# Two-block transformer on one core: positions loaded as columns, the compressing network's gelu written out with tanh, banded turns three steps later

## The chip, the cores and the metric

The kernel runs on one core of a Trainium2 chip, as five hand-written engine programs: TensorE (PE), VectorE (DVE), ScalarE (ACT), GpSimd (POOL) and SyncE (SP), which issues most of the DMAs. The metric is the device time of one execution in microseconds; lower is better.

## The reference

512 tokens of width 1024 in fp32 pass through two two-layer blocks. A layer of the first block mixes banded attention, a pooling mixer and MLA attention (which turns queries and keys by the positions), then a gated FFN. A layer of the second block has forgetting attention (fox) and sparse attention (NSA), whose compressed keys and values come out of a small network with a gelu.

```python
# first block, per layer; positions are 512 int32
ang = positions.astype(jnp.float32)[..., None] * inv_freq
cos, sin = jnp.cos(ang), jnp.sin(ang)
q_rope = apply_rope(q_rope, cos[:, :, None, :], sin[:, :, None, :])
k_rope = apply_rope(k_rope, cos, sin)
...
# swa_mixer: 6 query heads, 2 key heads, window 128, a bias by distance, sinks
q = rms_norm(q.reshape(B, S, SWA_HEADS, HEAD_DIM), q_gain)
k = rms_norm(k.reshape(B, S, SWA_KV_HEADS, HEAD_DIM), k_gain)
...
# second block, per layer, for keys (0) and values (1)
def compress_blocks(t, pos_emb, w1, b1, w2, b2):
    ...
    flat = blocks.reshape(B, G, nc, CMP_BLOCK * dh)
    return jax.nn.gelu(flat @ w1 + b1) @ w2 + b2
```

## The kernel before, in words

**Main parts and sides.** TensorE does every large product in fp32 as three matmuls of split parts (lines 667 to 669: high by high, low by high, high by low). A weight unit is loaded by SP into RAW, ScalarE makes the high part Wh (line 1520), VectorE the low part Wl (line 2283), both ahead of their use. Beside these main parts run "sides": generators for the small work (turns, i.e. transposes on TensorE, norms, attention items, the compressing network). At each step of the main part `tick` advances every open side to its next `yield`; `idle(n)` lets n steps go by. So the numbers in `idle` decide where in each engine's queue a small operation stands, and each engine works through its queue strictly in order. PSUM's eight banks go round: `fresh` waits until the bank's last reader is done (`bankN_drained`), a reader waits for `bankN_full`.

**Positions and angles.** SP loads the 512 positions as four rows POI[0:4, 128], last of 15 small loads that share the semaphore `gains_in`. VectorE casts them beside the gain rows (L2712), TensorE turns the gain rows (L1048) and the other rows with the positions (L1049), and VectorE copies the result into four columns of SS (L2718). Then VectorE begins the angles (L2743, L2745, L2747 into ANG), POOL carries them on in some 45 dependent operations (L3475 to L3506), with two DMAs of the bias table among them (L3534 waits for VectorE's VB, L2729). ScalarE takes the sine (L1828, L1829), and right behind it in its queue stands the copy of the values, V (L1847), which frees a bank that TensorE's main part waits for.

**POOL's first DMAs** wait for both halves of x (`x_in`), then come the 11 small loads of `small_in`; the last two are `b_forget`. TensorE's bias row (L1058) waits for all 11.

**Banded turns** (`window_side`). In each layer of the first block five 128-wide tiles of doubled keys (KD) and queries (QK) are turned on TensorE (L1032); ScalarE and VectorE take the high and low parts (KH, KL, QP) between MLA's attention items (L888 turns probabilities, L903 multiplies with values).

**The compressing network** (`keys_side(kv)`), in each layer of the second block for keys (kv 0) and values (kv 1): the hidden activations (64 blocks by 256) are turned on TensorE into "ht" (two tiles 128x64), ScalarE applies `Gelu_apprx_tanh` with the bias (L2141) into H1, TensorE multiplies by w2 (L1365). For the keys VectorE copies and rotates the result (KC, L3187 to L3193), TensorE turns it (L1373, "kct"), and KCHL takes its two parts.

Of the kernel before, what the change touches and what calls it, by code (L numbers as in the profile page):

```python
# [12 lines left out]
I32 = mybir.dt.int32  # L13
# [158 lines left out]
class Memory:  # L172

    def __init__(self, nc, ctx):
# [48 lines left out]
        self.POI = area("POI", [P], 9856, I32)  # L224
# [65 lines left out]
        self.H1 = area("H1", [2, 64], 20480)  # L290
        self.W2 = area("W2", [2, 2, 64], 20608)
# [48 lines left out]
class Signals:  # L340

    def __init__(self, nc, ctx):
        def sem(name):
            return ctx.enter_context(nc.semaphore(name))
# [6 lines left out]
        self.small_in = sem("small_in")  # L352
        self.blank = sem("gain_rows_blank")
# [60 lines left out]
        self.rk = sem("nsa_k_turned")  # L414
        self.h1 = sem("cmp_hidden_made")
# [222 lines left out]
N_GAINS, N_SMALL, N_NORMS = 15, 11, 4 * DEPTH  # L638
# [4 lines left out]
def tensor_program(pe, M, G, K, plan):  # L643
# [399 lines left out]
    def gains_side():  # L1043
        yield from idle(9)
        b = fresh("gains")
        pe.wait_ge(G.gains_in, 16 * N_GAINS)
        pe.wait_ge(G.set_up, 4)
        pe.transpose(b[:, 0:G_ROWS], M.GR[0:G_ROWS, :], ident[0:G_ROWS, 0:G_ROWS])  # L1048
        pe.transpose(b[:, 128:128 + 68], M.GR2[0:68, :], ident[0:68, 0:68]).then_inc(*K.fills("gains"))  # L1049
        K.close("gains")  # L1050
        yield from idle(3)
# [48 lines left out]
    def window_side(l):  # L1100
        yield from idle(24)
        while "bias" not in done:
            yield
        for j in (3, 4, 0, 1, 2):
            pe.wait_ge(G.win_k, 4 * l + 4)
            if j < 3:
                pe.wait_ge(G.win_n, NT * l + NT)
                turn_rows(f"win{l} {j}", lambda s: M.QK[:, s, j * P:(j + 1) * P])
            else:
                turn_rows(f"win{l} {j}", lambda s: M.KD[:, s, j - 3, :])  # L1110
            K.close(f"win{l} {j}")
            yield
            yield
# [147 lines left out]
    for l in range(DEPTH):  # L1261
# [89 lines left out]
        def keys_side(kv):  # L1351
            yield from idle(4)
            b = fresh(f"ht{l} {kv}")
            pe.wait_ge(*K.drained(f"hid{l} {kv}"))
            for j in range(2):
                i = pe.transpose(b[:, j * 64:j * 64 + 64], M.HT[0:64, j * P:j * P + P], ident[0:64, 0:64])
            i.then_inc(*K.fills(f"ht{l} {kv}"))
            yield
            K.close(f"ht{l} {kv}")
            yield from idle(3)  # L1360
            b = fresh(f"w2{l} {kv}")
            pe.wait_ge(*K.drained(f"ht{l} {kv}"))
            pe.wait_ge(G.w2_in, 32 * l + 32)
            for j in range(2):
                pe.matmul(b[0:64, 0:64], M.H1[:, j, :], M.W2[:, kv, j, :], start=j == 0, stop=False)  # L1365
            pe.matmul(b[0:64, 0:64], M.ONE[0:1, :], M.B2[0:1, 2 * l + kv, :], start=False, stop=True).then_inc(*K.fills(f"w2{l} {kv}"))
            yield
            if kv == 0:
                K.close(f"w2{l} {kv}")
                yield from idle(4)  # L1370
                b = fresh(f"kct{l}")
                pe.wait_ge(G.kc, l + 1)
                pe.transpose(b[:, 0:64], M.KC[0:64, :, :].rearrange("p a b -> p (a b)"), ident[0:64, 0:64]).then_inc(*K.fills(f"kct{l}"))  # L1373
                yield
# [127 lines left out]
def scalar_program(sc, M, G, K, plan, a):  # L1502
# [314 lines left out]
    def gains_side():  # L1817
        yield from idle(13)
        sc.wait_ge(G.set_up, 7)
# [39 lines left out]
    def window_side(l):  # L1859
        yield from idle(24)  # L1860
# [151 lines left out]
    for l in range(DEPTH):  # L2012
# [120 lines left out]
        def keys_side(kv):  # L2133
# [5 lines left out]
            for j in range(2):  # L2139
                col = G_B1 + 4 * l + 2 * kv + j  # L2140
                i = sc.activation(M.H1[:, j, :], M.bank[K.of(name)][:, j * 64:j * 64 + 64], ACT.Gelu_apprx_tanh, bias=M.GT[:, col:col + 1])  # L2141
            i.then_inc(*K.empties(name))
            yield from idle(4 if kv == 0 else 6)
            if kv == 0:
                yield from idle(5)
                upper(M.KCHL[:, :, 0, :], M.bank[K.of(f"kct{l}")][:, 0:64].rearrange("p (g n) -> p g n", n=32), f"kct{l}")
# [118 lines left out]
def vector_program(ve, M, G, K, plan):  # L2265
# [440 lines left out]
    def gains_side():  # L2706
# [10 lines left out]
        ve.tensor_copy(M.GT[:, G_ROWS:G_ROWS + 64], b[:, 128:192]).then_inc(G.set_up, 1)  # L2717
        ve.tensor_copy(PS4, b[:, 192:196]).then_inc(*K.empties("gains"))  # L2718
# [4 lines left out]
        ve.wait_ge(G.set_up, 7)  # L2723
# [95 lines left out]
    def window_side(l):  # L2819
# [7 lines left out]
        yield from idle(6)  # L2827
# [164 lines left out]
    for l in range(DEPTH):  # L2992
# [188 lines left out]
        def keys_side(kv):  # L3181
            yield from idle(9)
            name = f"w2{l} {kv}"
            b = M.bank[K.of(name)]
            if kv == 0:
# [8 lines left out]
                yield from idle(5)  # L3194
# [183 lines left out]
def sync_program(sp, M, G, K, plan, a, out):  # L3378
# [36 lines left out]
    sp.dma_start(M.POI[0:NT, :], a["positions"].rearrange("a (t p) -> (a t) p", p=P)).then_inc(G.gains_in, 16)  # L3415
# [21 lines left out]
def gpsimd_program(gp, M, G, K, a):  # L3437
# [164 lines left out]
```

## Time and profile before

| | |
|---|---|
| runs, us | 2717.89, 2719.95, 2719.98 (median 2719.95) |
| profiled execution, us | 2718.81 |
| its span, us | 2717.0 |
| PE busy | 2674.8 us, 98% |
| DVE busy | 1521.7 us, 56% |
| ACT busy | 1135.1 us, 42% |
| POOL busy | 210.0 us, 8% |
| TensorE's granted clock | 0.999 of 2.4 GHz |

The span runs from the first to the last instruction of the profiled execution; the time is 1.8 us longer. "Busy" adds up an engine's instructions, without waits. A row of the waits says which instruction waited, for what, how long in total, how many times, and the longest.

### The profile page before, as it was taken

Reading aid. Unit: us, or ns where it says so; the run is one execution under the profiler, and the core shown is the slowest. Engines: PE = TensorE matmul, PEld = TensorE weight load, DVE = VectorE, ACT = ScalarE, POOL = GpSimd, SP = SyncE. Lnnn points to the kernel's source line nnn. Section 1 sums busy time; section 2 is a strip of 40 time slices with the busy share of each in tenths; the row PEclk is TensorE's granted clock in tenths of the full one; section 3 lists DMA queues with packets and bytes.
Section 4 is the critical chain, followed back from the end, with each engine's and each line's share of the span. In section 5 each row is a group of like instructions: output and inputs, shape, how many; then the busy total and the mean of one; then the engine's idle time right before and its main releaser. Section 6 shows DMA issues by size and latency. Waiting matters only on the chain.

```text
span 2717.0 us, 34704 instructions
## 1 busy us (share of the span) xinstructions
PE 2674.8 (98%) x13449; PEld 2217.3 (82%) x13449; DVE 1521.7 (56%) x2678; ACT 1135.1 (42%) x2055; POOL 210.0 (8%) x323
## 2 busy tenths in 40 slices
PE   8999999999999999999999999999999999999999
PEld 7788888887888888878877888888878778888887
DVE  7756444467564444676776653343677776643343
ACT  4644222236542222455655343242465655342232
POOL 5200000002000000021122000000020121000000
PEclk9999999999999999999999999999999999999999
DMA  5113232321132333333311333333333212323332
GB/s 146 36 42 103 93 101 93 101 81 58 34 101 96 98 97 98 93 101 89 114 48 40 98 96 93 101 94 98 109 88 105 79 40 63 104 91 101 93 101 86
DMA packets 192279, 237.70 MB, mean 87 GB/s; under 512 B 12674, under 2 KB 145764, under 8 KB 192116
## 3 DMA queue, kind: packets, MB, share of 16 engines
q1 hardware_dynamic: 188852, 228.04, 27.9%
q0 software_dynamic: 2256, 5.52, 1.0%
q8 instruction: 108, 1.77, 0.3%
q10 hardware_dynamic: 1008, 1.92, 0.2%
q14 instruction: 55, 0.45, 0.0%
HBM read 227.05 MB, written 2.11 MB: 84 GB/s over the span
## 4 chain that ended last, share of the span: by engine, by line
PE 89%; DVE 5%; ACT 2%; POOL 1%; issue 1%; DMA 0%; SPq 0%; ACTq 0%; DVEq 0%; POOLq 0%
PE bank L667 26%; PE bank L669 26%; PE bank L668 26%; PE bank L958 2%; PE bank L903 1%; PE bank L979 1%; PE bank L980 1%; PE bank L1022 1%; PE bank L1021 1%; DVE Wl L2283 1%; PE bank L1223 1%; PE bank L888 1%; PE bank L1032 1%; PE bank L1421 1%; PE bank L1017 0%
## 5 line engine op out<-in xcount | busy, mean ns | idle before, releaser
L2283 DVE TENSOR_TENSOR Wl<-RAW,Wh 128x1024 fp32r<-128x1024 f32 (+4 forms) x434 | 511.5, 1201 | 326.0 <-ACT Wh L1520 325.1
L1520 ACT ACTIVATE Wh<-RAW 128x1024 fp32r<-128x1024 f32 (+4 forms) x434 | 438.1, 1032 | 397.6 <-PE bank L669 392.4
L667 PE MATMUL bank<-Hh,Wh 128*128 128x512 f32 x1104 | 448.3, 406 | 2.2 <-DVE Hl L2353 1.5
L669 PE MATMUL bank<-Hh,Wl 128*128 128x512 f32 x1104 | 431.7, 391 | 0.0
L668 PE MATMUL bank<-Hl,Wh 128*128 128x512 f32 x1104 | 431.0, 390 | 0.0
L667 PE MATMUL bank<-HA,Wh 128*128 128x512 f32 x704 | 274.2, 390 | 0.0
L669 PE MATMUL bank<-HA,Wl 128*128 128x512 f32 x704 | 273.9, 389 | 0.0
L668 PE MATMUL bank<-HA,Wh 128*128 128x512 f32 x704 | 273.9, 389 | 0.0
L669 PEld LDWEIGHTS bank<-Hh,Wl 128*128 128x128 f32 x1104 | 207.2, 188 | 45.0
L667 PEld LDWEIGHTS bank<-Hh,Wh 128*128 128x128 f32 x1104 | 208.3, 189 | 40.6 <-issue 4.8
L668 PE MATMUL bank<-A,Wh 128*128 128x512 f32 x608 | 236.5, 389 | 0.0
L667 PE MATMUL bank<-A,Wh 128*128 128x512 f32 x608 | 236.5, 389 | 0.0
L669 PE MATMUL bank<-A,Wl 128*128 128x512 f32 x608 | 236.5, 389 | 0.0
L668 PEld LDWEIGHTS bank<-Hl,Wh 128*128 128x128 f32 x1104 | 208.1, 188 | 33.6
L669 PEld LDWEIGHTS bank<-HA,Wl 128*128 128x128 f32 x704 | 132.1, 188 | 27.5
L668 PEld LDWEIGHTS bank<-HA,Wh 128*128 128x128 f32 x704 | 132.2, 188 | 27.3
L667 PEld LDWEIGHTS bank<-HA,Wh 128*128 128x128 f32 x704 | 132.1, 188 | 27.3
L2452 DVE TENSOR_TENSOR XT<-bank,XT 128x512 f32<-128x512 f32 x112 | 77.1, 690 | 121.6 <-PE bank L669 121.0
L1738 ACT ACTIVATE P<-bank,STT 128x384 f32<-128x384 f32 (+1 forms) x192 | 101.2, 527 | 96.7 <-DVE STT L2639 95.8
L667 PE MATMUL bank<-Wh,Hh 128*128 128x512 f32 (+3 forms) x384 | 139.4, 363 | 2.2 <-DVE Wl L2283 2.2
L2353 DVE TENSOR_TENSOR A<-TMP,A 128x512 fp32r<-128x512 f32 x108 | 74.8, 693 | 117.9 <-ACT A L1933 87.2
L669 PE MATMUL bank<-Wh,Hl 128*128 128x512 f32 (+3 forms) x384 | 134.6, 350 | 0.0
(408 smaller groups left out, 4711.3 us busy)
## 6 DMA issues: line engine op xcount, KB each, us to landing
RAW<-in_w_up_dram SPq DMA_DIRECT2D x108, 512.0 KB, 3.7
RAW<-in_w_down_dram SPq DMA_DIRECT2D x108, 512.0 KB, 3.7
RAW<-in_w_in_dram SPq DMA_DIRECT2D x86, 512.0 KB, 3.7
RAW<-in_w_gate_dram SPq DMA_DIRECT2D x44, 512.0 KB, 3.7
RAW<-in_w_out_dram SPq DMA_DIRECT2D x28, 512.0 KB, 3.7
RAW<-in_cmp_w_dram SPq DMA_DIRECT2D x16, 512.0 KB, 3.9
RAW<-in_w_o_fox_dram SPq DMA_DIRECT2D x8, 512.0 KB, 4.5
RAW<-in_w_o_nsa_dram SPq DMA_DIRECT2D x8, 512.0 KB, 3.5
```

The source lines that it names most:

```text
L667: pe.matmul(o, sh, mh, start=first, stop=False)
L668: pe.matmul(o, sh, ml, start=False, stop=False)
L669: return pe.matmul(o, sl, mh, start=False, stop=last)
L888: x = pe.transpose(b[:, k * P:(k + 1) * P], M.PB[:, i % 4, k * P:(k + 1) * P], ident)
L903: x = pe.matmul(b[:, h * 64:(h + 1) * 64], M.PT[:, i % 3, k * P:(k + 1) * P], values(g, h, kb[k]), start=k == 0, stop=k == len(kb) - 1)
L958: x = pe.transpose(b[:, k * P:(k + 1) * P], e[:, k * P:(k + 1) * P], ident)
L979: pe.matmul(b[:, c:c + w], v, ph, start=B.opens(n) and k == 0, stop=False, skip_group_check=True)
L1520: sc.activation(M.Wh[:, v % NHL, 0:n], M.RAW[:, v % NRAW, 0:n], ACT.Copy).then_inc(G.w_hi, 1)
L1738: sc.activation(e, M.bank[K.of(name)][:, 0:e.shape[1]], ACT.Exp, bias=M.STT[:, 0, t, h:h + 1], accum_out=M.STT[:, 1, t, h:h + 1]).then_inc ...
L2283: ve.tensor_tensor(M.Wl[:, v % NRAW, 0:n], M.RAW[:, v % NRAW, 0:n], M.Wh[:, v % NHL, 0:n].bitcast(F32), ALU.subtract).then_inc(G.w_lo, 1)
L2353: return ve.tensor_tensor(lo, src, h.bitcast(F32), ALU.subtract)
L2452: ve.tensor_tensor(M.XT[:, k, :], M.bank[K.of(name)][:, :], M.XT[:, k, :], ALU.add).then_inc(*K.empties(name))
```

## The change

It has three parts, which touch different stretches of the program.

1. **Positions.** Four DMAs of POOL load the positions straight into four columns (128 pieces of 4 bytes each), issued between the waits for the first and the second halves of x. The cast now makes the four columns of SS directly, and it and the three first angle operations stand in VectorE's queue ahead of the fourth Wl. The cast L2712, the copy L2718 and one of SP's loads go; the turn of the other rows has 64 rows in place of 68.
2. **Compressing network.** In place of the two gelus ScalarE takes h + b into HX (Identity) and its square into H1 (Square), VectorE makes (0.044715 x² + 1)·x, ScalarE the tanh, VectorE (0.5 t + 0.5)·x. The w2 matmuls and what follows stand later.
3. **Banded turns.** `window_side` begins three steps later on the three engines.

```diff
     def gains_side():          # TensorE
         yield from idle(9)
         pe.wait_ge(G.gains_in, 16 * N_GAINS)          # N_GAINS 15 -> 14
-        pe.wait_ge(G.set_up, 4)
+        pe.wait_ge(G.set_up, 3)
         pe.transpose(b[:, 0:G_ROWS], M.GR[0:G_ROWS, :], ident[0:G_ROWS, 0:G_ROWS])
-        pe.transpose(b[:, 128:128 + 68], M.GR2[0:68, :], ident[0:68, 0:68]).then_inc(*K.fills("gains"))
+        pe.transpose(b[:, 128:128 + 64], M.GR2[0:64, :], ident[0:64, 0:64]).then_inc(*K.fills("gains"))
...
     def window_side(l):        # TensorE, ScalarE; VectorE: idle(6) -> idle(9)
-        yield from idle(24)
+        yield from idle(27)
...
             K.close(f"ht{l} {kv}")   # TensorE, keys_side
-            yield from idle(3)
+            yield from idle(6)
             b = fresh(f"w2{l} {kv}")
-            pe.wait_ge(*K.drained(f"ht{l} {kv}"))
+            pe.wait_ge(G.h1, 2 * l + kv + 1)
...
                 K.close(f"w2{l} {kv}")
-                yield from idle(4)
+                yield from idle(6)
                 b = fresh(f"kct{l}")
...
             for j in range(2):       # ScalarE, keys_side
                 col = G_B1 + 4 * l + 2 * kv + j
-                i = sc.activation(M.H1[:, j, :], M.bank[K.of(name)][:, j * 64:j * 64 + 64], ACT.Gelu_apprx_tanh, bias=M.GT[:, col:col + 1])
+                h = M.bank[K.of(name)][:, j * 64:j * 64 + 64]
+                sc.activation(M.HX[:, j, :], h, ACT.Identity, bias=M.GT[:, col:col + 1])
+                i = sc.activation(M.H1[:, j, :], h, ACT.Square, bias=M.GT[:, col:col + 1])
             i.then_inc(*K.empties(name))
-            yield from idle(4 if kv == 0 else 6)
+            yield from idle(2)
+            sc.wait_ge(G.h_in, 2 * l + kv + 1)
+            sc.activation(M.H1[:, :, :], M.H1[:, :, :], ACT.Tanh, scale=float((2.0 / np.pi) ** 0.5)).then_inc(G.h_tanh, 1)
+            yield from idle(5 if kv == 0 else 7)
             if kv == 0:
-                yield from idle(5)
+                yield from idle(7)
...
     def gains_side():          # VectorE
-        yield from idle(7)
-        ve.wait_ge(G.gains_in, 16 * N_GAINS)
-        ve.tensor_copy(M.GR2[64:64 + NT, :], M.POI[0:NT, :]).then_inc(G.set_up, 1)
-        yield from idle(3)
+        yield from idle(10)
...
-        ve.tensor_copy(PS4, b[:, 192:196]).then_inc(*K.empties("gains"))
...
     def angle_side():          # VectorE
-        yield from idle(10)
+        yield from idle(3)
-        ve.wait_ge(*K.drained("gains"))
+        ve.wait_ge(G.pos_in, 16 * NT)
+        ve.tensor_copy(PS4, M.POI[:, :]).then_inc(*own.up())
+        ve.wait_ge(*own.now())
...
         def keys_side(kv):     # VectorE
-            yield from idle(9)
+            yield from idle(6)
+            ve.wait_ge(*K.drained(f"ht{l} {kv}"))
+            ve.tensor_scalar(M.H1[:, :, :], M.H1[:, :, :], 0.044715, 1.0, ALU.mult, ALU.add).then_inc(*own.up())
+            ve.wait_ge(*own.now())
+            ve.tensor_tensor(M.H1[:, :, :], M.H1[:, :, :], M.HX[:, :, :], ALU.mult).then_inc(G.h_in, 1)
+            yield from idle(2)
+            ve.wait_ge(G.h_tanh, 2 * l + kv + 1)
+            ve.tensor_scalar(M.H1[:, :, :], M.H1[:, :, :], 0.5, 0.5, ALU.mult, ALU.add).then_inc(*own.up())
+            ve.wait_ge(*own.now())
+            ve.tensor_tensor(M.H1[:, :, :], M.H1[:, :, :], M.HX[:, :, :], ALU.mult).then_inc(G.h1, 1)
+            yield from idle(4)
...
     for s in range(NT):        # POOL
-        for half in range(2):
-            gp.wait_ge(G.x_in[s][half], 16)
+        gp.wait_ge(G.x_in[s][0], 16)
+    for t in range(NT):
+        gp.dma_start(M.POI[:, t:t + 1], a["positions"][0, t * P:(t + 1) * P].rearrange("(p o) -> p o", o=1)).then_inc(G.pos_in, 16)
+    for s in range(NT):
+        gp.wait_ge(G.x_in[s][1], 16)
```

**Order, place 1.** VectorE's queue near the start, of before, from its copy of the diagonal masks (CMB) on; the first piece left out holds the low parts of x (Hl) and copies of its turned tiles (XT), the second also 13 small operations of the first norm.

```order
L2709 CAST CMB_65<-CST_61 128x128
L2283 TENSOR_TENSOR Wl_53<-RAW_52,Wh_54 128x832 [waits weights_hi_made]
...
L2712 CAST GR_31_79<-POI_80 4x128 [waits gains_in]
L2283 TENSOR_TENSOR Wl_53<-RAW_52,Wh_54 128x1024 [waits weights_hi_made]
...
L2718 COPY SS_71<-bank 128x4
L2720 TENSOR_SCALAR GT_62<-GT_62 128x2 [waits vector_own]
L2721 TENSOR_SCALAR GT_62<-GT_62 128x2
L2743 TENSOR_TENSOR ANG_81<-SS_71,CST_61 128x64 [waits bank1_drained]
L2745 TENSOR_SCALAR ANG_81<-ANG_81 128x64 [waits vector_own]
L2747 TENSOR_TENSOR ANG_81<-ANG_81 128x64 [waits vector_own]
L2729 TENSOR_TENSOR VB_76<-bank,INI_77 6x384 [waits bank2_full]
```

The same place of the change:

```order
L2718 CAST CMB_65<-CST_61 128x128
L2749 CAST SS_71<-POI_80 128x4 [waits positions_in]
L2751 TENSOR_TENSOR ANG_81<-SS_71,CST_61 128x64 [waits vector_own]
L2753 TENSOR_SCALAR ANG_81<-ANG_81 128x64 [waits vector_own]
L2755 TENSOR_TENSOR ANG_81<-ANG_81 128x64 [waits vector_own]
L2292 TENSOR_TENSOR Wl_53<-RAW_52,Wh_54 128x832 [waits weights_hi_made]
...
L2726 TENSOR_SCALAR GT_62<-GT_62 128x2 [waits vector_own,bank1_drained]
L2727 TENSOR_SCALAR GT_62<-GT_62 128x2
L2735 TENSOR_TENSOR VB_76<-bank,INI_77 6x384 [waits bank2_full]
```

The cast and the three angle operations moved from behind the gains to ahead of the fourth Wl (128x832), with the wait for the positions.

**Order, place 2.** VectorE's queue around the keys' network in the second block's first layer, of before; KSl is the low part of the selection's keys, M the mixing gate, STT the sums of the attention items.

```order
L2693 TENSOR_TENSOR KSl_144<-bank,KSh_143 64x512 x3
L2283 TENSOR_TENSOR Wl_53<-RAW_52,Wh_54 128x1024 [waits weights_hi_made]
L2499 TENSOR_TENSOR M_98_146<-bank,RBB_173 128x512 [waits bank5_drained,bank2_full]
L3187 COPY KC_156<-bank 64x64 [waits bank6_full]
...
L2499 TENSOR_TENSOR M_98_146<-bank,RBB_173 128x512 [waits bank5_drained,bank3_full]
L2283 TENSOR_TENSOR Wl_53<-RAW_52,Wh_54 128x1024 [waits weights_hi_made] x2
L2639 TENSOR_REDUCE STT_69<-bank 128x1 [waits bank4_full]
L2353 TENSOR_TENSOR KCHL_157<-bank,KCHL_157 128x2x32 [waits part_hi_made]
```

The same place of the change:

```order
L2292 TENSOR_TENSOR Wl_53<-RAW_52,Wh_54 128x1024 [waits weights_hi_made]
L3192 TENSOR_SCALAR H_106_154<-H_106_154 128x128 [waits bank1_drained]
L3194 TENSOR_TENSOR H_106_154<-H_106_154,HX_155 128x128 [waits vector_own]
L2702 TENSOR_TENSOR KSl_144<-bank,KSh_143 64x512 [waits part_hi_made]
L2702 TENSOR_TENSOR KSl_144<-bank,KSh_143 64x512 x3
L2292 TENSOR_TENSOR Wl_53<-RAW_52,Wh_54 128x1024 [waits weights_hi_made]
L3197 TENSOR_SCALAR H_106_154<-H_106_154 128x128 [waits cmp_hidden_tanh_made]
L3199 TENSOR_TENSOR H_106_154<-H_106_154,HX_155 128x128 [waits vector_own]
L2508 TENSOR_TENSOR M_98_146<-bank,RBB_174 128x512 [waits bank7_drained,bank2_full]
L2508 TENSOR_TENSOR M_98_146<-bank,RBB_174 128x512 [waits bank7_drained,bank5_full]
L2292 TENSOR_TENSOR Wl_53<-RAW_52,Wh_54 128x1024 [waits weights_hi_made]
L3205 COPY KC_157<-bank 64x64 [waits bank6_full]
```

The four new operations stand around the second group of KSl and a Wl; KC comes behind both M and a Wl, and KCHL, out of sight here, 18 rows later. On TensorE the w2 matmuls (L1365 before, L1369 now), which stood six products of three matmuls ahead of the first of the values' hidden products (bank<-Wh,XHL), now stand directly ahead of it.

**Order, place 3.** VectorE's queue at the banded turns of the first layer, of before; OS is an item's output, TMP its probabilities.

```order
L2354 SCALAR_TENSOR_TENSOR KL_91<-bank,GT_62,KH_90 128x512 [waits part_hi_made]
L2547 TENSOR_REDUCE STT_69<-bank 128x1 [waits bank1_full]
L2584 TENSOR_TENSOR OS_56<-bank,STT_69 128x384 [waits bank6_full,vector_own]
L2354 SCALAR_TENSOR_TENSOR QP_89<-bank,GT_62,QP_89 64x512 [waits part_hi_made] x2
L2560 COPY TMP_55<-bank 128x256 [waits bank6_full,bank4_full]
L2547 TENSOR_REDUCE STT_69<-bank 128x1 [waits bank5_full]
L2584 TENSOR_TENSOR OS_56<-bank,STT_69 128x384 [waits bank7_full,vector_own]
L2354 SCALAR_TENSOR_TENSOR QP_89<-bank,GT_62,QP_89 64x512 [waits part_hi_made] x2
L2547 TENSOR_REDUCE STT_69<-bank 128x1 [waits bank1_full]
L2354 SCALAR_TENSOR_TENSOR QP_89<-bank,GT_62,QP_89 64x512 [waits part_hi_made] x2
```

The same place of the change:

```order
L2363 SCALAR_TENSOR_TENSOR KL_91<-bank,GT_62,KH_90 128x512 [waits part_hi_made]
L2569 COPY TMP_55<-bank 128x256 [waits bank6_full,bank3_full]
L2556 TENSOR_REDUCE STT_69<-bank 128x1 [waits bank4_full]
L2593 TENSOR_TENSOR OS_56<-bank,STT_69 128x384 [waits bank7_full,vector_own]
L2363 SCALAR_TENSOR_TENSOR QP_89<-bank,GT_62,QP_89 64x512 [waits part_hi_made] x2
L2556 TENSOR_REDUCE STT_69<-bank 128x1 [waits bank2_full]
L2363 SCALAR_TENSOR_TENSOR QP_89<-bank,GT_62,QP_89 64x512 [waits part_hi_made] x2
L2569 COPY TMP_55<-bank 128x256 [waits values_mixed,bank3_full]
L2556 TENSOR_REDUCE STT_69<-bank 128x1 [waits bank4_full]
L2362 TENSOR_TENSOR Hl_51<-bank,Hh_50 128x3x128 [waits part_hi_made]
L2363 SCALAR_TENSOR_TENSOR QP_89<-bank,GT_62,QP_89 64x512 [waits part_hi_made] x2
```

Each of the five turns stands one attention item later; the three pairs of QP, which stood behind an OS, an OS and a reduction, now stand behind an OS, a reduction and an Hl.

## Rows read from the trace of the kernel before

**Rows 1.** The page: busy us, share of the span, instructions by engine.

```profile
PE 2674.8 (98%) x13449; PEld 2217.3 (82%) x13449; DVE 1521.7 (56%) x2678; ACT 1135.1 (42%) x2055; POOL 210.0 (8%) x323
```

**Rows 2.** Waits of TensorE, whole span: us in total, times, longest.

```profile
PE bank L958 <- POOL P L3455: 5.2, 8, 1.1
...
PE bank L667 <- ACT V L1847: 2.8, 1, 2.8
PE bank L667 <- DVE Wl L2283: 2.2, 2, 1.3
...
PE bank L1032 <- DVE QP L2354: 1.5, 2, 0.8
...
PE bank L1373 <- DVE KC L3193: 1.5, 2, 0.7
PE bank L888 <- DVE QP L2354: 1.4, 2, 0.7
```

**Rows 3.** Timeline of VectorE, start: start, duration, instruction, idle before and releaser.

```profile
19.45 1.03 DVE L2283 TENSOR_TENSOR Wl<-RAW,Wh 128x832 fp32r<-128x832 f32 x1 [2.13 <-ACT Wh L1520]
...
30.48 0.23 DVE L2747 TENSOR_TENSOR ANG<-ANG 128x64 f32<-128x64 f32 x1
30.62 0.54 DVE L2729 TENSOR_TENSOR VB<-bank,INI 6x384 f32<-6x384 f32 x1
```

**Rows 4.** Timeline of TensorE, start.

```profile
24.65 0.27 PE L1048 MATMUL bank<-CST,GR 96*128 96x96 f32 x1 [1.11 <-DVE GR L2712]
...
26.09 0.81 PE L1058 MATMUL bank<-INI,RB 32*6 32x384 f32 x2
```

**Rows 5.** DMA issues, 8 to 32 us: count, size, median us from issue to landing.

```profile
SS<-in_b_forget_dram POOLq DMA_DIRECT2D x2, 0.0 KB, 6.6
```

**Rows 6.** Timeline of POOL, 0 to 65 us.

```profile
13.19 0.76 POOL L3460 DMA_DIRECT2D INI<-in_cst_bias_dram  x1 [12.75 <-DMA XI<-in_x_dram]
...
18.17 1.03 POOL L3470 DMA_DIRECT2D SS<-in_b_forget_dram  x2
30.80 1.91 POOL L3493 TENSOR_SCALAR ANG<-ANG 128x128 f32<-128x128 f32 x1 [11.60 <-DVE ANG L2747]
...
35.25 0.60 POOL L3534 DMA_DIRECT2D bias_scratch<-VB  x1
...
64.52 0.32 POOL L3477 TENSOR_TENSOR ANG<-ANG 128x64 f32<-128x64 f32 x1
```

**Rows 7.** Timeline of ScalarE around the sine.

```profile
64.88 0.26 ACT L1828 ACTIVATE CSI<-ANG 128x64 f32<-128x64 f32 x1 [4.93 <-POOL ANG L3477]
...
65.18 1.12 ACT L1847 ACTIVATE V<-bank,SS 128x128 f32<-128x128 f32 x4
```

**Rows 8.** Timeline of ScalarE, the keys' network of the second block's first layer.

```profile
1317.27 1.28 ACT L2141 ACT_TABLE_LOAD   x1
1318.56 0.52 ACT L2141 ACTIVATE H<-bank,GT 128x64 f32<-128x64 f32 x2
...
1331.34 1.28 ACT L1738 ACT_TABLE_LOAD   x1
1333.41 0.69 ACT L1738 ACTIVATE P<-bank,STT 128x512 f32<-128x512 f32 x1 [0.78 <-DVE STT L2639]
```

**Rows 9.** Timeline of VectorE, the same stretch.

```profile
1322.35 2.80 DVE L2693 TENSOR_TENSOR KSl<-bank,KSh 64x512 fp32r<-64x512 f32 x4 [1.01 <-ACT KSh L1784]
1325.17 1.23 DVE L2283 TENSOR_TENSOR Wl<-RAW,Wh 128x1024 fp32r<-128x1024 f32 x1
...
1334.33 0.23 DVE L2353 TENSOR_TENSOR KCHL<-bank,KCHL 128x64 fp32r<-128x64 f32 x1 [0.96 <-ACT KCHL L1582]
```

**Rows 10.** Timeline of TensorE, the same stretch.

```profile
1326.04 0.28 PE L667 MATMUL bank<-Wh,XHL 128*64 128x256 f32 x1
...
1336.91 0.63 PE L958 MATMUL bank<-CST,P 128*128 128x128 f32 x4 [1.15 <-POOL P L3455]
```

**Rows 11.** Busy us (x instructions) by engine, clock, DMA share, in one stretch.

```profile
1386.00:1441.00 55.00, 51.49 (x312) 40.49 (x311) 41.35 (x103) 30.57 (x83) 14.07 (x23) 1.00 0.14 39
```

More of the change, by code:

```diff
@@ L223, in __init__ @@
         self.GR2 = area("GR2", [P], 9728)
-        self.POI = area("POI", [P], 9856, I32)
+        self.POI = area("POI", [NT], 9856, I32)
         self.ANG = area("ANG", [12, NT * 16], 20992)
@@ L290, in __init__ @@
         self.H1 = area("H1", [2, 64], 20480)
+        self.HX = area("HX", [2, 64], 23712)
         self.W2 = area("W2", [2, 2, 64], 20608)
@@ L352, in __init__ @@
         self.small_in = sem("small_in")
+        self.pos_in = sem("positions_in")
         self.blank = sem("gain_rows_blank")
@@ L414, in __init__ @@
         self.rk = sem("nsa_k_turned")
+        self.h_in = sem("cmp_hidden_cubed")
+        self.h_tanh = sem("cmp_hidden_tanh_made")
         self.h1 = sem("cmp_hidden_made")
@@ L635, in gain_column @@
     return (G_AN, G_FN, G_NM, G_NP)[2 * (n // 4) + n % 2] + 8 * (n % 4 // 2)
-N_GAINS, N_SMALL, N_NORMS = 15, 11, 4 * DEPTH
+N_GAINS, N_SMALL, N_NORMS = 14, 11, 4 * DEPTH
 FOX_WAIT = 6
@@ L1818, in gains_side @@
         yield from idle(13)
-        sc.wait_ge(G.set_up, 7)
+        sc.wait_ge(G.set_up, 5)
     def bias_side():
@@ L1859, in window_side @@
     def window_side(l):
-        yield from idle(24)
+        yield from idle(27)
         while "bias" not in done:
@@ L2716, in gains_side @@
         ve.tensor_copy(M.GT[:, 16:G_ROWS], b[:, 16:G_ROWS]).then_inc(*own.up())
-        ve.tensor_copy(M.GT[:, G_ROWS:G_ROWS + 64], b[:, 128:192]).then_inc(G.set_up, 1)
-        ve.tensor_copy(PS4, b[:, 192:196]).then_inc(*K.empties("gains"))
+        ve.tensor_copy(M.GT[:, G_ROWS:G_ROWS + 64], b[:, 128:192]).then_inc(*K.empties("gains"))
+        ve.wait_ge(*K.drained("gains"))
         ve.wait_ge(*own.now())
@@ L2722, in gains_side @@
         yield
-        ve.wait_ge(G.set_up, 7)
+        ve.wait_ge(G.set_up, 5)
     def bias_side():
@@ L2826, in window_side @@
         ve.tensor_copy(M.WS[:, :], M.RS[:, 0, 16:48]).then_inc(G.wf, 1)
-        yield from idle(6)
+        yield from idle(9)
         while "bias" not in done:
@@ L3193, in keys_side @@
                 ve.tensor_copy(M.KC[0:64, 1, :], M.KC[0:64, 0, :]).then_inc(G.kc, 1)
-                yield from idle(5)
+                yield from idle(7)
                 name = f"kct{l}"
@@ L3414, in sync_program @@
     sp.dma_start(M.GR2[0:64, :], a["cmp_pos_2"].rearrange("l k (m j) d -> (l k m) (j d)", j=2)).then_inc(G.gains_in, 16)
-    sp.dma_start(M.POI[0:NT, :], a["positions"].rearrange("a (t p) -> (a t) p", p=P)).then_inc(G.gains_in, 16)
     def cmp_input(l):
```

## The prediction, made blind

> **What bounds the kernel now.** I read the page's busy times first: TensorE is busy for 98% of the span, every other engine for 56% or less [rows 1]. So TensorE's matmuls are the floor, and the change, which leaves their number and sizes as they are (a 68-row turn becomes one of 64), can only move the time through the moments at which TensorE stands still. I therefore read TensorE's waits next. In 2717.0 − 2674.8 = 42.2 us TensorE is not busy, and the waits that the change touches are few and short [rows 2]: one wait of 2.8 us for ScalarE's V, one of 1.1 us for the cast of the positions [rows 4], one of 1.3 us of the two for Wl (at 86 us), 1.5 + 1.4 us at the banded turns (a pair in each of two layers), 1.5 us for KC (two layers), and the part of the 5.2 us for POOL's P that lies in the second block. The reader should see that 0.2% of 2720 us is 5.4 us: that is what a measurement of this kernel can tell from no change, and about the sum of what is to be had.
>
> The sum is made against the profiled execution: span 2717.0, time 2718.8. The median of the three runs is 2719.95, 1.1 above it.
>
> **Part 1, positions.** *The cast.* TensorE's turn of the gains starts at 24.65, after 1.11 us of waiting for the cast L2712 [rows 4], which VectorE reaches only after a queue of other work. In the change the turn needs only the landed gains and constants long made, and no VectorE operation stands between: the wait goes, −1.1. What is late next is the bias row, six matmuls further on (26.09 [rows 4]; it would be asked for at 25.0). It waits for POOL's small loads, the last of which is issued in a pair of 1.03 us from 18.17 [rows 6] and takes 6.6 us to land [rows 5], so at 18.7 + 6.6 = 25.3. A new wait of 0.3 appears (0 to 0.8): net −0.8.
>
> *The angles.* POOL starts them at 30.80, after 11.60 us of nothing, and ends at 64.52 + 0.32 = 64.84; ScalarE stands idle 4.93 us for them and then makes V, done at 66.3 [rows 6, 7]. TensorE waited 2.8 us of that [rows 2]. In the change VectorE has the first angles ready as soon as the positions are in, so POOL can begin after its last issue, 18.17 + 1.03 = 19.2. Five operations later it must issue the DMA of VB, at 35.25 before [rows 6]; this one waits for VectorE's VB, made at 30.62 + 0.54 = 31.16 [rows 3]. VectorE loses in front of it the cast, a copy and three angle operations (0.2 each by the row of 0.23 [rows 3]), so VB is done near 30.3, POOL issues at 30.4, 4.9 us earlier than before, and the remaining 29.6 us of chain (64.84 − 35.25) end at 59.9. Sine and V take 1.4 more: 61.3. TensorE asked for the bank at 66.3 − 2.8 = 63.5, and now, 0.8 earlier, at 62.7. The whole 2.8 goes, with 1.4 to spare. POOL's operations are uneven, one of 1.91 against a usual half [rows 6], so I keep 0 to −2.8 as bounds and take −2.8.
>
> *Behind it* comes the wait of 1.3 for Wl at 86 us [rows 2]. The chain behind the sine (V, keys, squares, VectorE's norms) starts some 5 us earlier, TensorE only 3.6; half of what feeds that chain is TensorE's own, so I take −0.6 (0 to −1.2).
>
> *The positions' landing.* POOL may issue once the first halves are in, at 13.19 at the latest [rows 6], and needs four issues of about 0.5 (half of the pair of 1.03). By the slowest of the small loads, 6.6 us [rows 5], they are in at 13.2 + 2.1 + 6.6 = 21.9 at the very worst; but 13.19 is the moment at which the second halves are in too, and the 6.6 were spent behind seven other loads in POOL's queue, while the positions are now its first. I take them as in by 18. VectorE has 2.13 us of idle ahead of the fourth Wl at 19.45 [rows 3], and the cast with three angle operations takes 0.9: free if the positions are in by 18.5. Cover gone, each microsecond later delays that Wl. I take 0, bound +2.
>
> The Trainium skill (DMA: Bandwidth & Descriptors, Rules for kernel authors) says that a non-contiguous last dimension lowers to one descriptor per element; here that is 512 pieces of 4 bytes, and it speaks against the change. The same page (Anatomy of one DMA) fits a POOL-issued DMA as 2.0 us plus bytes over 436 GB/s; by that fit the positions would be in well before 18 and the term stays 0. The only 4-byte loads here are the `b_forget` ones, with eight pieces each, and they take 6.6 us behind others in their queue [rows 5].
>
> Part 1: −0.8 − 2.8 − 0.6 = **−4.2**.
>
 Taken alone this is worth nothing: after the second load ScalarE still sat idle 0.78 for VectorE [rows 8], and TensorE's matmuls cover the first. Four small activations of about 0.26 (0.52 for two [rows 8]) and a tanh take their place. The Trainium skill (ScalarE: Activation LUTs, What ACT_TABLE_LOAD costs) adds a drain of 1.38 us to each load, which would make it 21.3 us in place of 10.3. In the trace the gelu begins 0.01 us after the load ends [rows 8], so none is seen behind the load, and the sum is the same by either.
>
> *The longer chain.* For w2 the activations now pass ScalarE, VectorE, ScalarE, VectorE. Two of VectorE's operations fit in its idle 1.01 ahead of KSl; the last two stand behind the Wl of 1325.17 to 1326.40 [rows 9]. ScalarE, without the load, hands over KSh some 0.5 earlier, which about pays for the first two, so I put the end of L3199 at 1326.3. TensorE, with the w2 matmuls (0.6) moved to directly ahead of XHL (1326.04 [rows 10]), asks for them at 1325.45: a new wait of 0.8 (0 to 1.5). The wait for KC, 0.7 per layer [rows 2], goes, for the turn stands far later. Between them the two leave +0.1 per layer.
>
> *Further on*, VectorE stood 0.96 for KCHL at 1334.33 [rows 9], and that delayed the sums that POOL's P needs, for which TensorE waited 1.15 at 1336.91 [rows 10]. KCHL now stands 18 rows later, so I take half, −0.5 per layer (0 to −0.9).
>
> *The clump.* From 1386 to 1441 TensorE is busy 51.49 of 55 us and VectorE 41.35 [rows 11]; the compressed scores run there beside turned probabilities, and come three steps later in the change. Which item meets which is shuffled; the 3.5 idle could fall to 2 or rise to 5, in each of two layers. I take 0, bounds ±3. The values' network has no wait of TensorE near it, so 0.
>
> Part 2: 2 × (0.1 − 0.5) = **−0.8**.
>
> **Part 3, banded turns.** TensorE waits 0.8 and 0.7 in each layer [rows 2], each time where a pair of QP (2 × 0.76 us) keeps VectorE from the item behind it. One item later the three pairs meet the same kind of neighbours, one of them an Hl. The pairs are no shorter and no farther apart, so I take 0, with −1.5 to +1 per layer.
>
> **Sum:** −4.2 − 0.8 + 0 = −5.0 us. 2718.8 − 5.0 = 2713.8; against the median 2719.95 it would be 2715.0. I say **2714.0**.
>
> **Rivals.**
> 1. *The shuffles pay* (parts 2 and 3). If the banded waits go (−2.9 in all) and the clump gives 1.5 per layer, it is −5 − 6 = −11: 2708. For: these waits are between small operations that a step moves. Against: VectorE is the engine waited for there, and its work has not shrunk. Chance 0.17.
> 2. *The sine comes hardly earlier.* If POOL's operations stretch by 3 us where they now overlap VectorE's other work, V's wait stays at about 1.6 and Wl's is unchanged: −5.0 + 1.6 + 0.6 = −2.8: 2716. For: the uneven row of 1.91. Chance 0.12.
> 3. *The positions land late.* Landing at 21 delays the fourth Wl and everything of VectorE behind it by 2.5, TensorE by some 2: −3.0: 2716. It is the case that the one-descriptor rule would make. Chance 0.06.
> 4. *Slower.* The clump turns bad: the compressed-score operations, three steps later, fall on the turned probabilities at which TensorE already waits [rows 11]. With eight of about 0.7 us per layer all uncovered, +11.2 − 5.0 = +6: 2725. It decides from 5.0 us of new waits on. Against: 13.6 us of VectorE are free in that stretch, more than the whole of it. Chance 0.06.
> 5. *The forecast*, 2714 ± 2.5: chance 0.59, and as the bound of 0.2% (2714.5 from the median) lies inside it, a little over half of it is faster.
>
> **Numbers.** Faster: 0.17 + 0.31 = 0.48; slower: 0.06; within 0.2%: the rest, 0.46. Range: down to rival 1 and up past rivals 2 and 3, 2708 to 2720.5.
>
> **What would show it.** The turn of the gains near 23.5 and the bias row near 25 with a short wait; POOL's angles from 19.2, their end near 60; no wait for V. Near 1325 a wait for H1 in place of that for KC; the wait for P about halved; 14 table loads in place of 22. Banded waits near 3 us in all. Wrong it would be by the clump above all, which I could only bound, and next by POOL's uneven durations.

## The result and the profile after

| | before | after |
|---|---|---|
| median us (20 runs each) | 2719.76 | 2725.23 |
| lowest to highest, us | 2717.89 to 2721.73 | 2719.62 to 2727.67 |
| profiled execution, us | 2718.81 | 2720.42 |
| its span, us | 2717.0 | 2718.6 |

The ratio is 1.0017, 95% interval 1.0011 to 1.0024: slower by 0.17%, where 2714.0 was forecast and 2708 to 2720.5 given as the range. The medians lie 5.5 us apart, the profiled executions 1.6: the changed kernel spreads over 8 us, and its profiled execution was its fourth fastest. The spread goes with TensorE's mean granted clock. Twelve of the 20 show a mean of 0.995 or 0.996, and lie at 2723.12 to 2727.67; the five fastest, at 2719.62 to 2722.52, show 0.997 to 0.999. The runs of before beside the experiments all show 0.998 or 0.999.

TensorE's waits after, as in [rows 2]:

```profile
PE bank L924 <- DVE QP L2363: 3.6, 3, 2.1
PE bank L962 <- POOL P L3472: 3.2, 4, 1.2
PE bank L1036 <- DVE QP L2363: 3.0, 2, 1.5
...
PE bank L1369 <- issue: 2.2, 2, 1.1
PE bank L1036 <- DVE KL L2363: 1.9, 4, 0.5
...
PE bank L1402 <- DVE CB L3268: 1.6, 2, 0.8
...
PE bank L1052 <- issue: 0.9, 1, 0.9
PE bank L671 <- DVE Wl L2292: 0.9, 1, 0.9
```

L667, L958, L1032 and L888 of before are now L671, L962, L1036 and L892; L924 is the turn of an attention output. The wait for V is gone, one for Wl is left of two, KC is gone. But the waits for the banded turns' parts (QP, KL) come to 3.6 + 3.0 + 1.9 = 8.5 us, where they were 2.9.

How far the changed kernel is ahead (−) or behind, matmul by matmul against before (the starts of the two traces' matmuls subtracted in order), where the difference has settled: −4.6 us at 95 us, −0.1 at 145, +6.1 at 700, +3.7 at 1500, +1.3 at 2500. So part 1 gained 4.6; the first layer's banded turns lost 4.5 and the second's 6.2; the second block's layers, with part 2, gained 2.4 each.

The second layer's turns, in stretches (columns as in [rows 11]):

```profile
674.00:680.00 6.00, 3.98 (x28) 3.19 (x27) 3.93 (x7) 3.52 (x9) 0.00 (x0) 0.97 0.01 1
680.00:690.00 10.00, 9.58 (x37) 7.46 (x36) 6.32 (x11) 5.38 (x13) 0.00 (x0) 0.50 0.01 2
690.00:700.00 10.00, 10.00 (x72) 8.69 (x71) 3.47 (x9) 3.80 (x12) 0.00 (x0) 1.00 0.00 0
```

The column to look at is PEclk. Between 674 and 680 TensorE was busy 3.98 of 6 us. Behind that, from 680 to 690, the granted clock stands at 0.50, the lower of its two levels (1.2 in place of 2.4 GHz). TensorE looks busy there, 9.58 of 10 us, and runs 37 matmuls; in the next ten microseconds it runs 72. In this execution the clock fell in the second layer alone; in turns_only below, with a mean of 0.996, it fell in both.

### The profile page after: what moved, and what is told of

It is laid out like the page before. It is cut to its first block, busy times and chain, and to the rows that moved or that the text cites. A ratio compares the mean times of both kernels' runs of the same rounds, so it can differ in the third digit from the quotient of the medians.

```text
span 2718.6 us, 34726 instructions
## 1 busy us (share of the span) xinstructions
PE 2677.7 (98%) x13449; PEld 2222.4 (82%) x13449; DVE 1523.3 (56%) x2693; ACT 1129.3 (42%) x2059; POOL 209.3 (8%) x327
## 4 chain that ended last, share of the span: by engine, by line
PE 94%; DVE 3%; ACT 1%; issue 1%; DMA 0%; POOL 0%; ACTq 0%; DVEq 0%; POOLq 0%
PE bank L671 27%; PE bank L673 27%; PE bank L672 27%; PE bank L962 2%; PE bank L907 1%; PE bank L983 1%; PE bank L1026 1%; PE bank L1025 1%; PE bank L984 1%; PE bank L1227 1%; PE bank L1036 1%; PE bank L892 1%; PE bank L1425 1%; PE bank L1021 1%; DVE Wl L2292 0%
## 5 line engine op out<-in xcount | busy, mean ns | idle before, releaser
L671 PE MATMUL bank<-Hh,Wh 128*128 128x512 f32 x1104 | 447.8, 406 | 2.3 <-DVE Hl L2362 1.5
L671 PE MATMUL bank<-HA,Wh 128*128 128x512 f32 x704 | 274.2, 390 | 0.0
L671 PEld LDWEIGHTS bank<-Hh,Wh 128*128 128x128 f32 x1104 | 208.2, 189 | 40.6 <-issue 4.8
L671 PE MATMUL bank<-A,Wh 128*128 128x512 f32 x608 | 236.5, 389 | 0.0
L671 PEld LDWEIGHTS bank<-HA,Wh 128*128 128x128 f32 x704 | 132.1, 188 | 27.2
L671 PE MATMUL bank<-Wh,Hh 128*128 128x512 f32 (+3 forms) x384 | 139.4, 363 | 0.9 <-DVE Wl L2292 0.9
```

Source lines behind the costliest of these rows:

```text
L671: pe.matmul(o, sh, mh, start=first, stop=False)
```

## The experiments

All are made from the two kernels. "Parts 1 and 2" is the changed kernel without part 3. Each median stands beside that of before on the same chip.

**Four splits.** Each takes whole parts of the change and nothing else:

```diff
# turns_only: before, and on TensorE and ScalarE
-        yield from idle(24)
+        yield from idle(27)
# and on VectorE idle(6) -> idle(9); pos_only, net_only: part 1 or 2 alone; no_turns: parts 1 and 2
```

> The kernel before with part 3 alone (the banded turns three steps later). Theory: this part is what costs. Its two stretches (120 to 131 us and 670 to 682 us) stand still some 4 us longer each, and in at least one of them the granted clock falls to its lower level in most executions: 2719.8 + 8 to 9 = 2728, up to 2732 where both fall, mean granted clock 0.995 to 0.998. Rival (the parts only cost together, because part 1 moves the first layer against the weights' loading): 2719 to 2722 and a clock of 0.999.

> The kernel before with part 1 alone (positions as columns, angles early). Theory: the shift of -4.6 us that the changed kernel has at 80 us stays to the end: 2715.3, clock 0.999, the turn of the gains still waiting about 1 us at 23.4. Rival (the gain is given back in the first layer's attention, whatever the turns do): 2719 to 2720.

> The kernel before with part 2 alone (the compressing network's activation from tanh, later w2 and keys). Theory: -2.1 us in the first and -2.5 us in the second of its two layers, as the changed kernel's shifts there: 2715.2, clock 0.999. Rival (those shifts come from the phase in which the changed kernel enters the stretch, not from part 2): 2719 to 2721.

> The changed kernel without part 3, so parts 1 and 2 together. Theory: the two gains add, -9.2 us: 2710.6, clock 0.999. Rival (the changed kernel's loss has a cause in part 1 or 2, such as 512 small pieces of DMA or longer chains): 2718 or more.

| kernel | median us (range) | before | ratio, 95% |
|---|---|---|---|
| turns_only | 2731.69 (2731.19 to 2742.12) | 2719.48 | 1.0052 (1.0039 to 1.0066) |
| pos_only | 2715.05 (2714.11 to 2717.12) | 2719.48 | 0.9984 (0.9975 to 0.9993) |
| net_only | 2714.41 (2713.84 to 2715.57) | 2719.48 | 0.9981 (0.9972 to 0.9990) |
| no_turns | 2710.81 (2709.43 to 2711.75) | 2719.48 | 0.9967 (0.9955 to 0.9979) |

The parts are separate: −4.4 and −5.1 alone, −8.7 together, and part 3 costs 12.2 alone and 14.4 on top of the others. The two rivals (parts that cost only together, gains that come from the phase) fall. no_turns is faster than both kernels. In turns_only the clock fell in both layers:

```profile
119.00:129.00 10.00, 7.50 (x56) 6.17 (x55) 6.16 (x13) 5.30 (x14) 0.00 (x0) 1.00 0.01 2
129.00:139.00 10.00, 9.60 (x38) 7.27 (x38) 6.09 (x12) 5.60 (x13) 0.00 (x0) 0.54 0.00 0
677.00:686.00 9.00, 6.55 (x50) 5.58 (x49) 5.67 (x12) 5.62 (x14) 0.00 (x0) 1.00 0.00 1
686.00:696.00 10.00, 9.49 (x36) 7.21 (x35) 6.32 (x11) 5.37 (x14) 0.00 (x0) 0.50 0.01 2
```

**Which engine's place it is** (all but the last on parts 1 and 2).

```diff
# evac_later: ScalarE and VectorE +3, TensorE as before
# evac_high_later: all three +1 (changes the order on ScalarE alone)
# turns_earlier: all three -3
# late_close: the changed kernel, and on TensorE
-            K.close(f"win{l} {j}")
             yield
             yield
+            K.close(f"win{l} {j}")
```

> Parts 1 and 2, and of part 3 only the ScalarE and VectorE side: the turns stand in TensorE's queue as before, their high and low parts (KH, KL, QP) three steps later. Theory A (the place of KL and QP in VectorE's and ScalarE's queues is what costs, since each pair of QP then stands between an exp and the next reduction): the loss of part 3 appears here in full, 2710.8 + 10 to 12 = 2722. Theory B (the place of the turns in TensorE's queue costs, because the turn takes a bank and a stretch of TensorE's cover away from narrower items): little of the loss here, 2711 to 2714.

> Parts 1 and 2 with all three numbers one step up instead of three. TensorE's and VectorE's orders stay as without part 3; only ScalarE's high parts stand one exp later. Theory A: part of the loss, since VectorE's low part waits for the later high part: 2713 to 2718. Theory B: no change, 2710.8 within 1.

> Parts 1 and 2 with the turns three steps earlier than before (21, 21 and 3 in place of 24, 24 and 6). If what costs is that later attention items are narrower and carry the output's turn beside them, going the other way gains or costs nothing: 2707 to 2711. If the place before was a fit by the step and any move loses: 2714 or more.

> The changed kernel with each turn's bank given back to the ring two steps later; the order on every engine is the same, only the bank numbers and so the waits for drained banks differ. If the loss is that a turn is handed the bank of the turn just ahead of it, it falls by half or more: 2714 to 2718. If it is the engines' own queues, no change: 2720 to 2727.

| kernel | median us (range) | before | ratio, 95% |
|---|---|---|---|
| evac_later | 2747.22 (2744.29 to 2752.94) | 2719.38 | 1.0104 (1.0089 to 1.0119) |
| evac_high_later | 2725.12 (2718.02 to 2729.05) | 2719.38 | 1.0017 (1.0008 to 1.0027) |
| turns_earlier | 2722.49 (2720.22 to 2727.01) | 2719.38 | 1.0013 (1.0003 to 1.0022) |
| late_close | 2724.96 (2720.66 to 2730.92) | 2719.38 | 1.0020 (1.0010 to 1.0030) |

Theory B fell: with TensorE's order untouched the loss is not smaller but larger (2747), and moving ScalarE's high parts behind one more exp makes as much of it (2725.1) as the whole of part 3. evac_high_later is the clean one of the two: against no_turns the order of instructions on TensorE, VectorE and POOL is the same from end to end, and on ScalarE only the high parts stand elsewhere. evac_later also pulls the turns and their parts apart. The size was missed too; both came out above what was expected of theory A, and neither expectation counted the clock: in evac_later it is 0.50 from 126 to 156 us, and evac_high_later with its clock up, at 2718.02, is at the upper end of what was expected. Here is the slowest execution of evac_high_later:

```profile
116.00:126.00 10.00, 6.54 (x49) 5.43 (x48) 7.11 (x15) 5.86 (x13) 0.00 (x0) 1.00 0.01 2
126.00:136.00 10.00, 10.00 (x40) 7.70 (x41) 5.05 (x10) 4.97 (x13) 0.00 (x0) 0.52 0.00 0
136.00:146.00 10.00, 10.00 (x39) 8.08 (x38) 2.00 (x5) 3.31 (x10) 0.00 (x0) 0.50 0.01 2
146.00:156.00 10.00, 9.61 (x58) 8.28 (x58) 4.16 (x12) 1.48 (x3) 0.00 (x0) 0.96 0.00 0
```

Its ten runs range from 2718.02, with a mean clock of 0.999, to 2729.05, with 0.994: the same instructions, 11 us apart. The bank ring (late_close) is not it: 2725.0 against 2725.2. And three steps the other way lose as well, 2722.5 against 2710.8: the expected 2707 to 2711 was wrong.

What sets the slow kernels apart can be counted in their traces. The same number of steps does not move the three engines by the same number of items: part 3 puts the turns and VectorE's low parts one item later, but ScalarE's high parts two exps later. Both layers of each trace give these counts, from the start of the layer's MLA attention; the last column is how long VectorE stood for ScalarE's KH and QP in the first layer.

| kernel | exps ahead of the first KH | reductions ahead of the first KL | median us | VectorE waits, us |
|---|---|---|---|---|
| before | 13 | 14 | 2719.8 | 0 |
| no_turns | 13 | 14 | 2710.8 | 0 |
| high_sooner (below) | 12 | 14 | 2710.7 | 0 |
| evac_high_later | 14 | 14 | 2725.1 | 5.1 |
| the changed kernel | 15 | 15 | 2725.2 | 4.1 |
| turns_only | 15 | 15 | 2731.7 | 4.0 |
| turns_earlier | 12 | 12 | 2722.5 | 5.2 |
| evac_later | 15 | 15 | 2747.2 | 3.3 |

An exp waits for the reduction of its own item. With 13 and 14 ScalarE makes the high part while VectorE still has one more reduction to do; with equal counts the high part can only be made after the very reduction behind which the low part stands. Every kernel that kept the lead is fast for its parts, every one that lost it is slow. (late_close, and filled below, have 15 and 15 too. turns_earlier has besides a wait of TensorE of 1.2 us for POOL's KD.) Part 3 with ScalarE's side one exp sooner, so that the lead is kept, was not run.

**The clock, and three single questions.**

```diff
# filled: the changed kernel, and on TensorE, ahead of the third QK turn (12) and of MLA's output turns (10);
# 32 a layer ran
+    def filler(count):
+        if spare:
+            for _ in range(count):
+                pe.transpose(M.bank[spare[0]][:, 384:512], ident, ident)
# gelu_kept: parts 1 and 2, gelu as before, later steps kept
# gains_later: parts 1 and 2, TensorE's gains_side
-        yield from idle(9)
+        yield from idle(12)
# high_sooner: parts 1 and 2, ScalarE's window_side
-        yield from idle(24)
+        yield from idle(22)
```

> The changed kernel with filler matmuls (each a 128x128 turn into spare columns of the bank that TensorE is filling) where TensorE stands still at the banded turns of both layers: 12 ahead of the third QK turn, 10 ahead of the next two output turns, 1.1 to 1.4 us each place, against waits of 1.5, 1.1 and 2.1 us. They do no useful work. Theory (half of the loss of part 3 is TensorE's granted clock, which falls after the stretch in which it stood still): the fall comes less often or not at all, mean granted clock 0.998 to 0.999 and a median of 2717 to 2721, below the changed kernel's 2725.2. Rival (the waits alone are the loss and the clock is a consequence without a price): 2725 or, by what the filler overshoots, 2727.

> Parts 1 and 2 without part 3, and of part 2 only the later steps: the gelu and its table loads stay, VectorE's four operations and the tanh go. Theory (part 2's gain comes from where KC, KCHL and the compressed scores stand, not from the eight table loads): 2710.8 as with the tanh, or up to 2 us less since the wait for the activations goes. Rival (the table loads, 10.3 us of ScalarE, are what was gained): 2714 to 2715, the time of part 1 alone.

> Parts 1 and 2 without part 3, TensorE's turn of the gain rows three steps (18 matmuls) later. Theory (its wait of 1 us at 23.4 was never the cast but the landing of the gain rows at 24.6): the wait goes and nothing follows it, 2710.8 - 1.0 = 2709.8. Rival (VectorE then waits for the turned gains and passes the wait on): 2710.8 or more.

> Parts 1 and 2, and of the banded turns only ScalarE's high parts (KH, QP) moved, one exp sooner; TensorE's and VectorE's orders stay. Theory (what matters is whether the high part stands ahead of or behind the exp that the next item needs; one place later cost 14): sooner makes the exp wait for TensorE's turn instead, and costs too, 2713 to 2722. Rival (later is bad, sooner is good, since VectorE's QP no longer waits): 2707 to 2710.

| kernel | median us (range) | before | ratio, 95% |
|---|---|---|---|
| filled | 2719.74 (2718.39 to 2720.90) | 2719.78 | 0.9999 (0.9990 to 1.0008) |
| gelu_kept | 2710.30 (2709.82 to 2713.22) | 2719.78 | 0.9967 (0.9954 to 0.9979) |
| gains_later | 2710.40 (2709.29 to 2712.22) | 2719.78 | 0.9965 (0.9953 to 0.9978) |
| high_sooner | 2710.70 (2709.37 to 2712.64) | 2719.78 | 0.9966 (0.9953 to 0.9978) |

filled is the telling one. Useless matmuls in the waits made the changed kernel 5.5 us faster and took its spread away (2.5 us in place of 8); all eleven runs show a mean clock of 0.999 or 1.000. Its timeline of TensorE at the third QK turn and the two output turns behind it:

```profile
122.73 1.48 PE L1039 MATMUL bank<-CST 128*128 128x128 f32 x12
124.30 0.66 PE L1046 MATMUL bank<-CST,QK 128*128 128x128 f32 x4
...
126.16 1.26 PE L1039 MATMUL bank<-CST 128*128 128x128 f32 x10
127.47 0.55 PE L927 MATMUL bank<-CST,OS 128*128 128x128 f32 x3
...
129.35 1.26 PE L1039 MATMUL bank<-CST 128*128 128x128 f32 x10
131.62 0.55 PE L927 MATMUL bank<-CST,OS 128*128 128x128 f32 x3 [1.01 <-DVE QP L2374]
```

L1039 is the filler. The turns behind it start at 124.30, 127.47 and 131.62, where the changed kernel's, without filler, start at 124.44, 127.52 and 131.67:

```profile
124.44 0.63 PE L1036 MATMUL bank<-CST,QK 128*128 128x128 f32 x4 [1.50 <-DVE QP L2363]
...
127.52 0.55 PE L924 MATMUL bank<-CST,OS 128*128 128x128 f32 x3 [1.09 <-DVE QP L2363]
...
131.67 0.55 PE L924 MATMUL bank<-CST,OS 128*128 128x128 f32 x3 [2.11 <-DVE QP L2363]
```

So the filler ends no wait sooner; it only keeps the engine going through it, and what follows runs at the full clock:

```profile
672.00:680.00 8.00, 6.96 (x51) 5.69 (x51) 5.45 (x10) 4.75 (x12) 0.00 (x0) 1.00 0.01 3
680.00:690.00 10.00, 8.94 (x69) 7.54 (x68) 6.96 (x13) 5.87 (x15) 0.00 (x0) 1.00 0.00 0
```

Beside the changed kernel's 37 matmuls in 680 to 690, these are 69, of them 20 filler. The Trainium skill (TensorE: Matmul & The Clock Gate, Part 1) says that the array is throttled by default and that activity releases it; these rows agree that work keeps the clock up, and no row here shows what the default is. By filled, the clock's share of the loss is 5.5 us, and what is left to no_turns (2719.74 − 2710.81 = 8.9 us, from two chips) is the waits themselves. Two other numbers say the same: the first layer of the changed kernel's trace, whose clock held, lost 4.5 us, twice which is 9.0; and the fastest of the changed kernel's 20 runs, with a mean clock of 0.999, is 2719.62.

gelu_kept: 2710.3 with the table loads still in the program. The rival fell: the 10.3 us of loads that part 2 removes gain nothing that can be measured, and its 5 us come from where the later operations stand. gains_later: 2710.4 against 2710.8, inside the spread. high_sooner: 2710.7, no difference; that a sooner high part costs was wrong, and that it gains was too: a lead of two items is worth no more than a lead of one.

## Why the prediction was wrong

**Part 1, predicted −4.2, measured −4.4: right in sum, partly by luck, with two of its terms mis-sized.** In the changed kernel's trace the shift against before is +0.3 behind the turn of the gains (−0.8 forecast), −3.3 from V's place (−2.8) and −1.6 at the wait for Wl (−0.6); the two misses cancel. V's wait went whole, as forecast. POOL began at 19.01, waited for VB (8.42 us) and ended near 59.3; the forecast had 19.2 and 59.9:

```profile
19.01 0.57 POOL L3513 TENSOR_SCALAR ANG<-ANG 128x128 f32<-128x128 f32 x1 [0.15 <-issue]
...
30.98 0.61 POOL L3554 DMA_DIRECT2D bias_scratch<-VB  x1 [8.42 <-DVE VB L2735]
...
58.78 0.53 POOL L3497 TENSOR_TENSOR ANG<-ANG 128x64 f32<-128x64 f32 x1
```

The positions were in time: POOL issued their four DMAs from 7.82, they took 5.1 us to land (the median of the four), and the cast ran at 17.23. The rival of late positions fell. The fourth Wl came at 19.92 in place of 19.45 [rows 3], after a wait for ScalarE's Wh and not for the positions, and TensorE waited for neither. The wait at 86 us went whole. The turn of the gains did not move: 24.65 before [rows 4], 24.68 after, with 0.94 us of idle ahead of it, although no cast stands before it any more. This step failed: the row named the cast as the releaser, since it came last, and with the cast gone a wait of nearly the same length stayed. What ends it now is not shown. The landing of the gain rows is the likely cause, argued from the equal times alone, and gains_later could not settle it: in no_turns TensorE came to the turn at 25.41 and did not wait.

**Part 2, predicted −0.8, measured −5.1: right in direction, mis-sized.** The wait for the activations came as forecast (1.1 per layer, 0.8 forecast), and the one for KC went. The mis-sized term is "the clump", taken as 0 with bounds of ±3 per layer. With part 2 (no_turns):

```profile
PE bank L962 <- POOL P L3472: 1.6, 2, 1.2
PE bank L1402 <- DVE CB L3268: 0.8, 1, 0.8
PE bank L1025 <- DVE PT L2362: 0.4, 2, 0.2
```

in 1386 to 1441, 2.8 us in all where before had 1.4 + 1.4 + 0.6 = 3.4, with wholly other waits among them: the four between 1386 and 1396 went, the one for the scores (CB) and a longer one for P came. Matmul by matmul, net_only gains 0.8 us by 1345, where 0.4 was forecast, and 1.7 more from there to 1450; the second layer repeats both. Of the 1.7 the waits are only 0.6. The rest is busy time: the same 614 matmuls take 100.4 us in place of 101.5 there, and why is not shown.

By 1345 the sum came near for another reason than the one given. The wait for P at 1336.9 [rows 10] went whole, but not because KCHL stands later: gelu_kept has KCHL late and no wait for the activations, and there TensorE waits 1.2 for P again. The new wait ahead of w2 takes the old one's place, since TensorE now comes to P that much later; the prediction counted the two as independent. That table loads are worth nothing in the time was right, and gelu_kept shows it.

**Part 3, predicted 0, with +1 per layer as the upper bound, measured +12 to +14: the step that failed.** The prediction said that "the pairs are no shorter and no farther apart", and so the waits stay. It counted VectorE's work and its neighbours, and not whom VectorE waits for. [rows 2] gave 1.5 + 1.4 us of waits for QP, at a VectorE that was never idle ahead of a pair. Around the first pair of before, from the timelines of VectorE and ScalarE:

```profile
120.73 0.56 DVE L2547 TENSOR_REDUCE STT<-bank 128x1 f32<-128x384 f32 x1 [0.41 <-PE bank L1017]
121.32 0.58 ACT L1679 ACTIVATE TMP<-bank,STT 128x384 f32<-128x384 f32 x1 [0.72 <-DVE STT L2547]
121.90 1.38 ACT L1582 ACTIVATE QP<-bank,GT 64x512 fp32r<-64x512 f32 x2
122.22 0.42 DVE L2547 TENSOR_REDUCE STT<-bank 128x1 f32<-128x256 f32 x1 [0.20 <-PE bank L1017]
...
123.77 1.51 DVE L2354 SCALAR_TENSOR_TENSOR QP<-bank,GT,QP 64x512 fp32r<-64x512 f32 x2
```

A reduction stands between, and the high part is ready. After, the same place and the two behind it:

```profile
120.92 0.55 DVE L2556 TENSOR_REDUCE STT<-bank 128x1 f32<-128x384 f32 x1
...
121.50 0.58 ACT L1683 ACTIVATE TMP<-bank,STT 128x384 f32<-128x384 f32 x1 [1.61 <-DVE STT L2556]
...
122.07 1.38 ACT L1586 ACTIVATE QP<-bank,GT 64x512 fp32r<-64x512 f32 x2
122.78 1.51 DVE L2363 SCALAR_TENSOR_TENSOR QP<-bank,GT,QP 64x512 fp32r<-64x512 f32 x2 [0.85 <-ACT QP L1586]
...
125.95 1.51 DVE L2363 SCALAR_TENSOR_TENSOR QP<-bank,GT,QP 64x512 fp32r<-64x512 f32 x2 [1.20 <-ACT QP L1586]
...
129.51 0.56 DVE L2362 TENSOR_TENSOR Hl<-bank,Hh 128x384 fp32r<-128x384 f32 x1 [1.12 <-ACT Hh L1586]
```

VectorE now stands idle ahead of the first two pairs, for ScalarE's high part, and ahead of the Hl before the third. That part stands in ScalarE's queue behind an exp, and the exp waits for VectorE's reduction of the same item, which stands behind the pair before. So the two queues take turns where they used to overlap, and TensorE, which waits for the banks that VectorE frees, loses 1.1 to 2.1 us at each of the three places. The prediction's "one item later" holds for TensorE and VectorE; ScalarE's high parts moved two exps, and their lead of one item was lost. evac_high_later shows that ScalarE's place alone suffices, and the counts above that the lost lead is common to all slow kernels.

The second half of the step, that a stall costs its own length and no more, failed as well: no sentence of the prediction spoke of the granted clock. The waits cost 8.9 us and the clock 5.5 more.

The rival "slower" named 2725, the time that was measured, and that is luck: it put the slowdown in the clump and asked for 5 us of new waits there, where the waits fell by 0.6 per layer. "The shuffles pay" was right for part 2 (1.5 per layer from the clump, 1.7 measured) and wrong for part 3.

## What to carry to other kernels

A short wait of the busiest engine can have two prices, its length and the clock behind it: before a small operation is moved in a stretch where TensorE already waits in every item or two, look at the granted clock of the stretch after, in several executions, since a spread between equal runs can be the clock falling or not. When a group of operations is moved by the same number of steps on several engines, count on each engine how many items it passes, and check that whoever prepares for another keeps its lead. Follow the wait one engine further than the one that the row names; here the engine that was waited for was itself about to wait. Measure the parts of a change apart: two of these three gained 8.7 us together, and the third hid it.

## What the runs showed of the hardware

Filler matmuls in waits of 1.1 to 2.1 us, 32 a layer, made a kernel 5.5 us faster. In turns_only and in the changed kernel's second layer the clock fell although no single wait of TensorE there was longer than 1.5 us; in the changed kernel's first layer it held with one of 2.1. TensorE was busy 7.50 of 10 us before a fall in turns_only (119 to 129) and 6.54 of 10 in evac_high_later; but in the changed kernel's first layer it was busy 7.78 of 13 us (119 to 132) before none. So these runs give no amount of work at which it falls, and the same place fell in some executions and not in others. Executions of one program on one chip differed by 11 us with it. Four POOL DMAs of 128 pieces of 4 bytes took 5.1 us to land while x and the weights were loading, and part 1 as a whole still came out at its forecast. ScalarE's eight table loads of 1.28 us, off the path of TensorE, were worth nothing that these runs can measure (2710.3 with them, 2710.8 without).
